# A transformer block kernel: attention steps placed elsewhere between the projection chunks, and the gate sigmoids moved into the gate chunks

## The reference, cut to what matters

```
h = rmsnorm(x, norm_mix_g)
proj = h @ w_in                       # 1024 -> 7424 columns
qkv_a, q_b, k_b, v_b, gate_logits = split(proj)
# branch A: 3 groups (window, dilation) x 8 heads of 64; q and k get rmsnorm and a partial rotation
#   masked attention in each group, the three groups joined by their softmax denominators
# branch B: 8 query heads, 2 key/value heads; q and k get rmsnorm and an axial rotation
gates = sigmoid(gate_logits.reshape(b, s, 2, d) + b_gate)
merged = gates[:, :, 0] * (o_a @ w_proj_a) + gates[:, :, 1] * (o_b @ w_proj_b)
x = x + merged @ w_out
```

## Time and profile before

| | |
|---|---|
| median of 3 runs | 2184.15 us |
| profiled execution, its own time | 2184.15 us |
| its span from first to last instruction | 2182.3 us |
| mean granted TensorE clock | 0.972 |
| PE busy | 2053.9 us, 94% |
| DVE busy | 973.7 us, 45% |
| ACT busy | 282.7 us, 13% |

### The profile page before, as it was taken

How to read it: one execution, slowest core, us unless ns; L and a number is a source line. 1 busy time by engine, 2 the same in 40 slices (tenths; PEclk the granted TensorE clock), 3 DMA queues, 4 the chain that set the end, 5 groups by cost and what they waited for, 6 DMA issues and landing times.

```text
span 2182.3 us, 24192 instructions
## 1 busy us (share of the span) xinstructions
PE 2053.9 (94%) x9832; PEld 1235.6 (57%) x9832; DVE 973.7 (45%) x1570; ACT 282.7 (13%) x508; POOL 88.0 (4%) x107
## 2 busy tenths in 40 slices
PE   7999999999999999999999999988789997988997
PEld 4456655444344444443444447858768885766885
DVE  3322324333333333223333325645667676667765
ACT  1122221001011110001011013111100100211000
POOL 2210000000000000000000000104200000000000
PEclk9999998999999999999999999998989998999998
DMA  9432124899999999999999993331115453424551
GB/s 368 152 116 95 66 97 156 348 427 428 428 428 428 428 428 428 428 428 428 428 428 428 428 422 119 116 116 39 58 60 193 168 197 135 155 77 174 174 202 49
DMA packets 106012, 560.12 MB, mean 257 GB/s; under 512 B 5856, under 2 KB 11232, under 8 KB 81248
## 3 DMA queue, kind: packets, MB, share of 16 engines
q1 hardware_dynamic: 102528, 551.61, 63.0%
q10 hardware_dynamic: 3424, 7.67, 1.0%
HBM read 558.21 MB, written 1.05 MB: 256 GB/s over the span
## 4 chain that ended last, share of the span: by engine, by line
PE 70%; DMA 19%; DVE 7%; issue 2%; POOL 1%; ACT 1%; ACTq 0%; SPq 0%; POOLq 0%; DVEq 0%
DMA ring<-in_w_gate_up_dram 19%; PE ps L945 13%; PE ps L702 11%; PE ps L984 7%; PE ps L985 7%; PE ps L986 7%; PE ps L971 5%; PE ps L920 3%; PE ps L1033 2%; PE ps L908 2%; PE ps L1041 1%; PE ps L1113 1%; PE ps L738 1%; PE ps L771 1%; PE ps L1127 1%
## 5 line engine op out<-in xcount | busy, mean ns | idle before, releaser
L945 PE MATMUL ps<-ring,arena 128*64 128x512 f32 x2048 | 451.8, 596 | 8.9 <-DMA ring<-in_w_gate_up_dram 8.9
L945 PEld LDWEIGHTS ps<-ring,arena 128*64 128x64 f32 x2048 | 143.0, 137 | 301.5 <-issue 277.4
L1984 DVE TENSOR_SCALAR arena<-ps 128x512 f32<-128x512 f32 x32 | 22.1, 692 | 505.6 <-PE ps L945 505.6
L984 PE MATMUL ps<-split_w,act_parts 128*128 128x512 f32 (+1 forms) x544 | 217.1, 399 | 25.7 <-DVE act_parts L1601 25.7
L702 PE MATMUL ps<-ring,actT 128*128 128x512 f32 (+1 forms) x544 | 236.3, 585 | 1.6 <-DMA ring<-in_w_in_dram 1.5
L971 PE MATMUL ps<-ring,arena 128*64 128x512 f32 x1024 | 226.8, 595 | 0.0
L985 PE MATMUL ps<-split_w,act_parts 128*128 128x512 f32 (+1 forms) x544 | 212.5, 391 | 0.0
L986 PE MATMUL ps<-split_w,act_parts 128*128 128x512 f32 (+1 forms) x544 | 212.0, 390 | 0.0
L1601 DVE TENSOR_TENSOR split_w<-ring,split_w 128x2048 fp32r<-128x2048 f32 (+2 forms) x92 | 198.1, 2153 | 3.2
L702 PEld LDWEIGHTS ps<-ring,actT 128*128 128x128 f32 x544 | 100.0, 190 | 114.0 <-issue 111.0
L971 PEld LDWEIGHTS ps<-ring,arena 128*64 128x64 f32 x1024 | 70.7, 137 | 133.3 <-issue 133.3
(11 more groups left out here) (298 smaller groups left out, 2085.9 us busy)
## 6 DMA issues: line engine op xcount, KB each, us to landing
ring<-in_w_gate_up_dram SPq DMA_DIRECT2D x128, 2048.0 KB, 21.9
ring<-in_w_down_dram SPq DMA_DIRECT2D x64, 2048.0 KB, 19.8
ring<-in_f_w_dram SPq DMA_DIRECT2D x28, 2048.0 KB, 7.9
ring<-in_w_in_dram SPq DMA_DIRECT2D x14, 2048.0 KB, 11.0
ring<-in_a_w_in_dram SPq DMA_DIRECT2D x8, 2048.0 KB, 7.9
ring<-in_b_w_qkv_dram SPq DMA_DIRECT2D x6, 2048.0 KB, 7.9
ring<-in_f_w_dram SPq DMA_DIRECT2D x4, 1536.0 KB, 6.9
ring<-in_w_out_dram SPq DMA_DIRECT2D x2, 2048.0 KB, 7.7
```

The source lines that it names most:

```text
L945: mm = pe.matmul(ps[half, bank, :], xeT[:, 2 * c + j, :], w[:, j, at:at + 512], start=False, stop=(c == 3 and j == 1), skip_group_check=True)
L984: pe.matmul(dst, lh, rh, start=start, stop=False)
L1984: dve.tensor_scalar(gate_c, ps[:, 1, :], 7.0, None, ALU.min).then_inc(m_gate, 1)
```

## The change

It has two parts. In `first_timeline` the attention steps 0 to 9 no longer follow the halves of chunks 8 to 10. One step follows each of chunks 3 to 10, behind both tiles and, for chunks up to 7, behind the turn of the heads of tile 0; chunks 9 and 10 have a second step directly after the first. Steps 10 to 25 stay where they were. In the second part the sigmoid of a gate product is taken by ACT as soon as DVE has added its bias, in eight instructions of 512 columns, and the four instructions behind the output copies go away. DVE waits for eight signals instead of four before its first multiply by a gate.

```diff
--- before.py
+++ after.py
@@ -133,13 +133,22 @@
     events, step = [], 0
     for c in range(len(W_CHUNKS)):
         for tile in range(NT):
-            for half in range(2):
-                events.append(("half", c, tile, half))
-                if half and c - (tile == 0) in HEAD_CHUNKS and (c, tile) != (0, 0):
-                    events.append(("turn_heads", c - (tile == 0), 1 - tile))
-                if c >= 11 or c in (8, 9) and (tile, half) != (0, 0) or c == 10:
-                    events.append(("attend", step))
-                    step += 1
+            events.append(("half", c, tile, 0))
+            if c >= 11:
+                events.append(("attend", step))
+                step += 1
+            events.append(("half", c, tile, 1))
+            if c - (tile == 0) in HEAD_CHUNKS and (c, tile) != (0, 0):
+                events.append(("turn_heads", c - (tile == 0), 1 - tile))
+            if c >= 11:
+                events.append(("attend", step))
+                step += 1
+        if 3 <= c <= 10:
+            events.append(("attend", step))
+            step += 1
+            if c >= 9:
+                events.append(("attend", step))
+                step += 1
     while step < UNITS + 2:
         events.append(("attend", step))
         step += 1
@@ -1336,6 +1345,11 @@
                     elif kind == "v_a":
                         act.activation(v_a[:, tile, group * 512:(group + 1) * 512], ps[:, bank, :],
                                        ACT.Copy).then_inc(gemm_free[bank], 1)
+                    else:
+
+                        act.wait_ge(gemm_free[bank], g // GB + 1)
+                        s = gates[:, tile, group * 512:(group + 1) * 512]
+                        act.activation(s, s, ACT.Sigmoid).then_inc(gates_ready, 1)
                 elif event[0] == "turn_heads":
                     kind, group, _, _ = W_CHUNKS[event[1]]
                     tile = event[2]
@@ -1375,12 +1389,6 @@
                                ps[:, 4 + 2 * b, :].rearrange("p (c s) -> p c s", s=P), ACT.Copy)\
                     .then_inc(oT_ready, 1)
 
-            for g in range(G_PROJ - 3, G_PROJ):
-                read_out(act, g)
-            for b in range(2):
-                for tile in range(NT):
-                    s = gates[:, tile, D - b * D:2 * D - b * D]
-                    act.activation(s, s, ACT.Sigmoid).then_inc(gates_ready, 1)
             act.dma_start(late[:, 0:9 * P], t["late"]).then_inc(late_in, 16)
             gu_rows = t["b_gate_up"].rearrange("e (b h n) -> h e b n", b=2, h=2)
             for q in range(4):
@@ -1784,7 +1792,7 @@
                                 ps[:, 5 + 2 * b, :].rearrange("p (c s) -> p c s", s=P))\
                     .then_inc(oT_ready, 1)
 
-            dve.wait_ge(gates_ready, 4)
+            dve.wait_ge(gates_ready, 8)
             g = G_PROJ
             for tile in range(NT):
                 for n in range(2):
```

## The result

The changed kernel takes 2215.09 us (median of four runs, 2214.71 to 2216.74) against 2184.59 us (median of four, 2181.64 to 2190.09): a ratio of 1.0138, 95% interval 1.0117 to 1.0158, some 30 us slower. I had forecast 16.5 us more, 2200.6 us, and a range up to 2208. Sign and waits were right; nearly half of the loss was not in the sum.

The account below looks back on a forecast made before the run. The prediction took PE as the bound, busy 236.78 of 237.00 us from 60 to 297 us. Waits of 12.6 + 4.6 less 0.7 made 16.5 us, added to 2184.15: 2200.6 us, range 2194 to 2208.

Parts of the forecast that it names:

- (a): Scores of steps 2, 3, 4, behind chunks 5, 6, 7: PE waits for DVE's multiply behind head work, 12.6 us in all.
- (b): Steps 7 and 9, directly behind 6 and 8: PE waits for the exponential, 2.2 and 2.4 us, sum 4.6.
- (c): PE's list of chunk halves and steps: six fewer interruptions give back 0.7 us, bounds 0 and 1.0.
- Part 2, cost 0: Sigmoids moved into the gate chunks: added sigmoids and table loads on ACT cost PE 0; gain 0, at most 1 us.
- The rival of the table loads: Gate chunks: a load costs 2.57 us, not 1.28, making PE wait; 9.9 us more, 2210.5 us, chance 0.06.
- The clock: Rival at the new gaps: granted clock falls, 6 us once or 18 for three, 2207 to 2219 us; chance 0.05.
- The prediction's own sign of being wrong: From 60 to 320 us: PE's idle time grows by less than 12 or more than 22 us, or the clock leaves 1.00.
- The price of a fall: Behind the new gaps: each fall of the clock, taken as a 12 us stretch, costs 6 us more.
- the worst case: The clock rival's upper end: three falls in the new gaps, 18 us more, 2219 us.
- PE's time is its list of instructions and every wait is added: From 60 to 297 us: PE is busy 236.78 of 237.00 us, so each new wait adds to the total.

Follow-up runs that it names:

- d_dve_first: The changed kernel, but DVE alone takes its part of steps 0 to 4 ahead of the heads of (chunk, tile 1): 2196.64 us, ratio 1.0043.
- g_dve_first_split: The changed kernel with DVE's part of steps 0 to 4 ahead of its head work, and one step behind each tile of chunks 9 and 10: ratio 1.0001.
- b_sigmoids_only: The kernel before with only the sigmoids moved into the gate chunks, attention steps as before: ratio 0.9997.
- a_steps_only: The changed kernel with the sigmoids left behind the output turns, so only the attention steps move: 2215.06 us, ratio 1.0131.
- e_fill_heads: The changed kernel with four unread products before the scores of steps 2, 3 and 4, none before steps 7 and 9: 2209.30 us, ratio 1.0096.
- f_fill_less: The changed kernel with two unread products before the scores of steps 2, 3, 4 and two before the weighted products of steps 7, 9: 2208.07 us, ratio 1.0096.
- i_before_fill: The kernel before with three unread products ahead of the second turn of heads: ratio 0.9999.
- j_router_fill: The kernel before with unread products added ahead of the counting of experts (three instead of two) and the product awaiting the flags (two more): 2181.65 us, ratio 0.9983.

## Why the prediction was wrong, step by step

- *(a) The waits for `o_ready`, 3 x 4.2 us:* right, place, releaser and size (12.9). d_dve_first shows that DVE's head work makes them.
- *(b) The waits for the exponential, 4.6 us:* right (4.5). g_dve_first_split has neither these nor (a) and is back at the time of before.
- *(c) Interruptions, 0.7 us back:* not found. Without waits and falls g_dve_first_split takes 239.2 us for the stretch that took 239.0. The sum left out that a product behind a step takes 6.97 us and one behind a turn of heads alone 6.87 (89.52 to 96.39), so that the five steps now in the head stage add 0.1 us each. The size is within the error of every whole time.
- *Part 2, cost 0:* right (b_sigmoids_only). The rival of the table loads is out: the load takes 1.28 us and the next instruction starts at once, eight times over. The drain that the Trainium skill adds to a switch ("ScalarE: Activation LUTs", "What ACT_TABLE_LOAD costs") is not seen between instructions here; by that figure an estimate of the cost is some 11 us, and b_sigmoids_only measures -0.7 us (-2.8 to 1.3).
- *The clock, "the new gaps are a fifth of their stretch, so I expect none", chance 0.05:* this step failed. It was a term of the sum, not a rival to it: 13.3 us in five places. The reasoning failed in two ways. I compared a single gap of 4.2 us with the busy share of a longer stretch, whose idle time was one wait of 2.76 us, and I took one profiled execution as proof: at 28 to 36 us the clock stood at 1.00 in the kernel before, yet with the same instructions it fell there in the kernel after (the two rows at the end of this section). The prediction's own sign of being wrong came true: PE's idle time grew as forecast, and the clock left 1.00.
- *The price of a fall* was also read badly: 6 us each, from the 12 us stretch of the earlier trace rows. They cost 1.7 to 4.6 each. With three of my price I had 2219 as the worst case; the true time lies inside that rival by luck, since five falls of 2.7 us on average make up for three of 6, and outside a range that gave it almost no room.
- *"PE's time is its list of instructions and every wait is added":* true for the waits, and incomplete. The list itself has no fixed length: the same instructions kept PE busy for 12 us more.

The two rows of the kernel after, columns as in the earlier trace rows:

```profile
32.00:36.00 4.00, 2.46 (x10) 2.14 (x11) 2.72 (x13) 0.60 (x1) 0.94 (x2) 0.81 1.04 386
36.00:40.00 4.00, 4.00 (x14) 3.01 (x14) 0.37 (x2) 0.61 (x3) 0.00 (x0) 0.77 1.05 387
```

What stays open: why a wait of 2.1 us in front of step 7 is followed by a low clock in the changed kernel's profile and not in d_dve_first's, and in which places the slower executions of every kernel, which spread over some 8 us, lose their clock.

## What to carry to other kernels

When an edit puts a wait of a few microseconds in front of a saturated TensorE, price it as the wait plus the slower work behind it: here 17.4 us of waits brought 13.3 us more. When one list orders several engines, look for each moved step at what the *other* engine has ahead of its part at that moment; a step moved "into free time" here landed behind 5.7 us of another engine's queue. If a wait can't be removed, unread matmuls in it are worth trying, as long as they end before the signal. A clock of 1.00 in one profiled execution does not show that a place is safe.

## What the runs showed of the hardware

Around waits that left PE idle for 4.3 us in one piece the granted clock fell in three places of three in the profile of the changed kernel, and in that of a_steps_only; for idle pieces of 2.1 to 2.5 us it fell in some and not in others (both in the changed kernel, in a_steps_only and in e_fill_heads, one of two in d_dve_first, one of three in f_fill_less). Behind the wait of 2.75 us ahead of the second turn of heads, which every kernel but i_before_fill has with the same instructions on PE, it fell in four profiles of eleven (the changed kernel, a_steps_only, g_dve_first_split and j_router_fill). For 0.8 us it fell in none. A fall lasted some 3 to 10 us at 0.50 (the shortfall of the clock in its 4 us stretches, divided by 0.5), and the five of the changed kernel cost 1.7 to 4.6 us each. Products that nothing reads kept the clock at 1.00 in all five places, and in a stretch of small dependent matmuls they gave 3.7 us to a kernel that had two such products already.
